# Encoder layer on one core: pool group folded into the output weights, row scales stored in runs of 16 bytes

## What is computed

```
z = rms_norm(x) @ w_in                 # columns: pool group u (512) | q (512) | k | v
# pool group, 4 groups of 128 channels, windows 2/4/8/16
m[g] = centred_mean(u[g]) - u[g]
pool_out[g] = (m[g] @ pool_w[g]) * pool_scale[g]
attn_out = softmax(q k^T / 8) v        # 8 query heads of 64, 2 key heads, q and k normed and rotated
x = x + rms_norm(concat(pool_out, attn_out) @ w_out)
x = x + rms_norm((silu(h @ w_gate) * (h @ w_up)) @ w_down),  h = rms_norm(x)
x = x + (p @ w_ple_proj) * sigmoid(x @ w_ple_gate + b)
```

## Time and profile before

| | us |
|---|---|
| median of 3 runs | 2368.6 |
| lowest, highest | 2368.44, 2368.7 |
| profiled execution, span | 2371.2 |
| attention, first scores to last values | about 395 |

### The profile page before, as it was taken

One profiled execution on the slowest core, in us unless ns is written; L12 is line 12 of the kernel. 1 busy time (PEld: TensorE's weight loads), 2 busy tenths in 40 slices (PEclk: granted clock), 3 DMA queues, 4 the chain that ended last, 5 costly groups with the idle time before them and its releaser, 6 DMA issues.

```text
span 2371.2 us, 29645 instructions
## 1 busy us (share of the span) xinstructions
PE 2305.7 (97%) x10928; PEld 1907.5 (80%) x10928; DVE 1684.8 (71%) x1754; ACT 1038.1 (44%) x1539; POOL 951.7 (40%) x557
## 2 busy tenths in 40 slices
PE   8999999999999989999999999899999999999999
PEld 7888787877778868888887888788788888877877
DVE  5766788888755687676766555888889965575852
ACT  4433788888744453333333222444343333233221
POOL 0000345555423655444443566344456534550210
PEclk9999999999999999999999999999999999999999
DMA  5222233232268884453547867564457587676432
GB/s 198 72 73 97 87 59 74 61 54 59 49 159 246 246 252 161 138 173 122 171 141 262 305 254 263 163 219 163 155 199 260 196 325 265 249 244 236 147 120 75
DMA packets 333550, 402.75 MB, mean 170 GB/s; under 512 B 32736, under 2 KB 236512, under 8 KB 333280
## 3 DMA queue, kind: packets, MB, share of 16 engines
q1 hardware_dynamic: 333408, 400.87, 51.9%
HBM read 259.18 MB, written 137.43 MB: 167 GB/s over the span
## 4 chain that ended last, share of the span: by engine, by line
PE 80%; DVE 8%; DMA 5%; issue 3%; ACT 2%; POOL 1%; SPq 1%; POOLq 0%; DVEq 0%; ACTq 0%
PE ps L1424 46%; PE ps L1213 29%; PE ps L1216 5%; DMA row_scales<-recip 2%; DVE ring L2179 1%; DVE reg L2187 1%; DMA scales<-row_scales 1%; DMA xb<-x_turned 1%; DVE negmax L2083 1%; DMA f_turned<-ev 1%; DVE atb L2097 0%; DVE pt L2125 0%; DVE fhi L2299 0%; DMA ff_forms<-fhi 0%; ACT pt L1529 0%
## 5 line engine op out<-in xcount | busy, mean ns | idle before, releaser
L1424 PE MATMUL ps<-reg,ring 128*128 128x512 f32 x5544 | 1271.0, 391 | 27.0 <-DVE ring L2179 17.7
L1424 PEld LDWEIGHTS ps<-reg,ring 128*128 128x128 f32 x5544 | 1045.5, 189 | 251.2 <-DVE ring L2179 22.0
L1529 ACT ACTIVATE ring<-wraw 128x1024 fp32r<-128x1024 f32 (+2 forms) x152 | 143.7, 946 | 389.5 <-PE ps L1424 389.5
L2179 DVE TENSOR_TENSOR ring<-wraw,ring 128x1024 fp32r<-128x1024 f32 (+2 forms) x152 | 232.2, 1528 | 63.4 <-ACT ring L1529 62.6
L1213 PE MATMUL ps<-win,ht 128*128 128x512 f32 (+1 forms) x1152 | 228.2, 359 | 8.5 <-DVE win L2053 8.3
L1213 PEld LDWEIGHTS ps<-win,ht 128*128 128x128 f32 x1152 | 191.1, 191 | 39.3 <-DVE ht L2010 7.3
L1529 ACT ACTIVATE ring<-ws 128x1024 fp32r<-128x1024 f32 (+2 forms) x114 | 108.0, 947 | 253.3 <-PE ps L1424 236.3
L2179 DVE TENSOR_TENSOR ring<-ws,ring 128x1024 fp32r<-128x1024 f32 (+2 forms) x114 | 175.0, 1535 | 43.2 <-ACT ring L1529 42.6
L2125 DVE TENSOR_TENSOR pt<-ps,pt 128x512 fp32r<-128x512 f32 x256 | 173.6, 685 | 40.5 <-ACT pt L1529 37.6
L1213 PE MATMUL ps<-wout,ct 128*128 128x512 f32 x768 | 180.6, 393 | 2.0 <-DVE wout L2106 1.7
L1529 ACT ACTIVATE pt<-ps 128x512 fp32r<-128x512 f32 x256 | 153.3, 600 | 56.7 <-PE ps L1216 55.9
(11 more groups left out here) (205 smaller groups left out, 2921.4 us busy)
## 6 DMA issues: line engine op xcount, KB each, us to landing
reg<-ff_forms SPq DMA_DIRECT2D x42, 1536.0 KB, 10.0
ff_forms<-fhi SPq DMA_DIRECT2D x88, 512.0 KB, 3.2
wraw<-in_w_gate SPq DMA_DIRECT2D x88, 256.0 KB, 4.2
wraw<-in_w_up SPq DMA_DIRECT2D x88, 256.0 KB, 4.7
ff_forms<-ev SPq DMA_DIRECT2D x44, 512.0 KB, 2.9
wraw<-in_w_down SPq DMA_DIRECT2D x48, 384.0 KB, 5.4
reg<-ff_forms SPq DMA_DIRECT2D x14, 1024.0 KB, 6.8
xt_a<-in_xt SPq DMA_DIRECT2D x16, 512.0 KB, 4.5
```

The lines of the kernel that those rows point to most:

```text
L1424: last = nc.tensor.matmul(ps[:, 2 * chain + m, :], ring[:, st % 3, a, m, k * P:(k + 1) * P], reg[:, k, i, e, :], start=OPENS[i] and k == 0 ...
L1529: copy = lambda out, src, **k: nc.scalar.activation(out, src, ACT.Copy, **k)
L2179: V.tensor_tensor(ring_block(u, st, 1), weight_source(u, i), f(ring_block(u, st, 0)), ALU.subtract).then_inc(S["w_split"], 1)
```

## The change

1. The store of the reciprocals keeps each partition's four values together: `r_d` is (128, 4) in place of (4, 128), so a row is stored in 128 runs of 16 bytes, not 512 of 4 bytes. The order in the row of 512 differs, and `o_scale` reads it with a step of four elements.
2. `pool_w[g]`, times `pool_scale` and turned by the host's layout, is multiplied with rows g of `w_out` once, in the projection (`fold`, g = 0 to 3: two halves of 512 columns, 3 matmuls each, into banks 5 and 6 behind the Q columns of tiles 3 to 6). ACT and DVE split the raw strip (`fold_hi`, `fold_split`), ACT takes the product (`fold_back`), SP loads and stores it in `out_folded`, which the output strips 0 to 3 are then read from.
3. In the attention PE's and ACT's `pooled` and POOL's split are gone; POOL writes the centred mean straight into `plb`.

```diff
@@ misc_schedule
-        order.append(("pool", h))
@@ DRAM
+    wf_d = nc.dram_tensor("out_folded", (NPOOL, P, D), F32, kind="Internal").ap()
-    r_d = nc.dram_tensor("row_scales", (2 * NSEQ * NH, 4, P), F32, kind="Internal").ap()
+    r_d = nc.dram_tensor("row_scales", (2 * NSEQ * NH, P, 4), F32, kind="Internal").ap()
@@ SP
-                sp.dma_start(out_place(k), w_out[k * P:(k + 1) * P, :]).then_inc(S[f"strip_in{k}"], 16)
+                rows = wf_d[k] if k < NPOOL else w_out[k * P:(k + 1) * P, :]
+                sp.dma_start(out_place(k), rows).then_inc(S[f"strip_in{k}"], 16)
+            def fold_in(g):
+                sp.wait_ge(S["strip_split"], KT)
+                sp.wait_ge(S["fold_split"], g)
+                sp.dma_start(fold_raw[:], w_out[g * P:(g + 1) * P, :]).then_inc(S["fold_in"], 16)
                 rows_in(n)
+                if 3 <= n < 3 + NPOOL:
+                    fold_in(n - 3)
+                if 5 <= n < 5 + NPOOL:
+                    sp.wait_ge(S["fold_out"], n - 4)
+                    sp.dma_start(wf_d[n - 5], fold_out[:]).then_inc(S["fold_st"], 16)
-                    sp.dma_start(r_d[hc].rearrange("t p -> p t"), recip[:, hc % 2]).then_inc(on("scales_out"), 16)
+                sp.dma_start(r_d[hc], recip[:, hc % 2]).then_inc(on("scales_out"), 16)
-                sp.dma_start(scales[own_rows(hc)], r_d[hc].rearrange("t p -> (t p)").partition_broadcast(HD))\
+                sp.dma_start(scales[own_rows(hc)], r_d[hc].rearrange("p t -> (p t)").partition_broadcast(HD))\
-                sp.wait_ge(S["misc_free"], MISC[("pool", job)] + 1)
+                sp.wait_ge(S["m_ready"], job + 1)
@@ POOL, windows
-                go(nc.gpsimd.tensor_tensor(m[:, 8:520], s[:, 8:520],
-                                           u[:, PAD + t0:PAD + t0 + 512], ALU.subtract))
-                go(nc.gpsimd.tensor_copy(mt_hl[:, 0, :], m[:, 8:520]))
-                nc.gpsimd.tensor_tensor(mt_hl[:, 1, :], m[:, 8:520], mt_hl[:, 0, :].bitcast(F32),
-                                        ALU.subtract).then_inc(S["m_ready"], 1)
+                pool.wait_ge(*at_least(f"pl_out{hf}", 16 * (job // 2)))
+                nc.gpsimd.tensor_tensor(plb[:, hf], s[:, 8:520],
+                                        u[:, PAD + t0:PAD + t0 + 512], ALU.subtract).then_inc(S["m_ready"], 1)
@@ PE
+            def fold(g):
+                pe.wait_ge(S["fold_split"], g + 1)
+                pe.wait_ge(S["u_stored"], g + 3)
+                pe.wait_ge(S["k_stored"], g + 3)
+                for c in range(2):
+                    for m, (a, b) in enumerate(((0, 0), (0, 1), (1, 0))):
+                        last = mm(ps[:, 5 + c, :], poolw[:, a, g, :], fold_hl[:, b, c * 512:(c + 1) * 512],
+                                  m == 0, m == 2)
+                last.then_inc(S["fold_done"], 1)
                 columns(n, Q)
+                if 3 <= n < 3 + NPOOL:
+                    fold(n - 3)
-                if u == 7:
-                    pooled(h)
@@ ACT
+            def fold_hi(g):
+                act.wait_ge(S["fold_in"], 16 * (g + 1))
+                act.wait_ge(S["fold_done"], g)
+                copy(fold_hl[:, 0], fold_raw[:]).then_inc(S["fold_hi"], 1)
+            def fold_back(g):
+                act.wait_ge(S["fold_done"], g + 1)
+                act.wait_ge(S["fold_st"], 16 * g)
+                copy(fold_out[:], pair(5)).then_inc(S["fold_out"], 1)
                 q_root(n)
+                if 3 <= n < 3 + NPOOL:
+                    fold_back(n - 3)
+                if 2 <= n < 2 + NPOOL:
+                    fold_hi(n - 2)
-                copy(plb[:, half], ps[:, 7, :], scale=pscale[:, k:k + 1]).then_inc(S["misc_free"], 1)
@@ DVE
                 q_rows(n)
+                if 2 <= n < 2 + NPOOL:
+                    dve.wait_ge(S["fold_hi"], n - 1)
+                    V.tensor_tensor(fold_hl[:, 1], fold_raw[:], f(fold_hl[:, 0]), ALU.subtract)\
+                        .then_inc(S["fold_split"], 1)
-                V.tensor_tensor(atb[rows, hc % 2], atb[rows, hc % 2], scales[rows], ALU.mult).then_inc(on("o_scaled"), 1)
+                t = atb[rows, hc % 2].rearrange("p (t n) -> p t n", t=4)
+                V.tensor_tensor(t, t, scales[rows].rearrange("p (n t) -> p t n", t=4), ALU.mult)\
+                    .then_inc(on("o_scaled"), 1)
```

More of the change, by code:

```diff
@@ L564, in scales_through @@
                 sp.wait_ge(*at_least("scales_made", hc + 1))
-                with nc.allow_non_contiguous_dma(reason="512 scales, from columns to a row"):
-                    sp.dma_start(r_d[hc].rearrange("t p -> p t"), recip[:, hc % 2]).then_inc(on("scales_out"), 16)
+                sp.dma_start(r_d[hc], recip[:, hc % 2]).then_inc(on("scales_out"), 16)
             def scales_in(hc):
@@ L1015, in windows @@
                 grp, hf = job % NH // 2, job % 2
+                if job:
+                    pool.wait_ge(S["m_ready"], job)
+                    alone(pool)
                 u = chan[:, grp, :]
@@ L1326, in pv @@
                     last.then_inc(S["pv_done"], 1)
-            def pooled(job):
-                misc(("pool", job))
-                pe.wait_ge(S["m_ready"], job + 1)
-                for m, (a, b) in enumerate(((0, 0), (0, 1), (1, 0))):
-                    last = mm(ps[:, 7, :], poolw[:, a, job % NH // 2, :], mt_hl[:, b, :], m == 0, m == 2)
-                last.then_inc(S["misc_done"], 1)
             turn_q(0, 0)
@@ L1614, in _ @@
                 strip(k)
-            act.wait_ge(S["pw_raw"], 16)
-            copy(poolw[:, 0].rearrange("p g n -> p (g n)"), qtok[:].rearrange("p h d -> p (h d)"))\
-                .then_inc(S["early_hi"], 1)
+            act.wait_ge(S["pw_raw"], 32)
+            raw = qtok[:].rearrange("p h d -> p (h d)")
+            for g in range(NPOOL):
+                last = copy(poolw[:, 0, g], raw[:, g * P:(g + 1) * P], scale=pscale[:, g:g + 1])
+            last.then_inc(S["early_hi"], 1)
             square(0)
@@ L2059, in _ @@
             dve.wait_ge(S["early_hi"], 2)
-            V.tensor_tensor(poolw[:, 1].rearrange("p g n -> p (g n)"),
-                            qtok[:].rearrange("p h d -> p (h d)"),
-                            f(poolw[:, 0]).rearrange("p g n -> p (g n)"), ALU.subtract).then_inc(S["early_lo"], 1)
+            raw = qtok[:].rearrange("p h d -> p (h d)")
+            for g in range(NPOOL):
+                last = V.scalar_tensor_tensor(out=poolw[:, 1, g], in0=raw[:, g * P:(g + 1) * P],
+                                              scalar=pscale[:, g:g + 1], in1=f(poolw[:, 0, g]),
+                                              op0=ALU.mult, op1=ALU.subtract)
+            last.then_inc(S["early_lo"], 1)
             norm(0)
```

92 lines of the change are left out of this document (54 added, 38 removed).

## The result

| | before | after |
|---|---|---|
| median of the runs beside each other | 2368.1 us (7 runs) | 2376.3 us (7 runs) |
| ratio | | 1.0038, 95% interval 1.0028 to 1.0048 |
| profiled execution, span | 2371.2 | 2374.7 |

The change makes the kernel about 9 us slower; 14 us faster had been forecast. On two other chips the ratio came out at 1.0048 and 1.0045, so this is no matter of one chip.

A forecast was written before the change was run, and what follows sets the result against it. PE's own work, and whatever makes DVE late in the attention (`o_scale`), were taken as the bound; 5.5 - 11.2 + 4.2 - 3.7 - 1.7 - 4.0 - 3.2 = -14.1 us, to 2354.5; range 2346 to 2366.

The forecast's parts named there:

- At nothing: List of changes priced at 0, among them small `poolw` passes, loads, semaphores and `o_scale` reading with a step of four.
- The slower rival: `o_scale` on DVE at u = 3 and 7 pays for its step; gain gone from about 0.55 us on; 6%.
- fold, PE's work: Projection: 24 added matmuls of 512 columns at 0.2275 us each on a full PE, +5.5 us.
- fold, waits: Projection: operands and copies have cover and SP's late loads do not reach PE; 0, up to 5 us.
- pooled matmuls: Attention: three matmuls fewer on PE in each of 16 heads, 0.70 us a head, -11.2 us.
- given back at u = 7: Attention: PE, now earlier, waits about 0.28 us for DVE's low part in 15 heads, +4.2 us (0 to 10.5).
- waits behind late DMAs, clock: Attention: two PE waits behind late DMAs go, -3.7 us, and the clock fall near 598 us, -1.7 us.
- collisions with POOL: Attention: POOL's shorter, earlier windows no longer slow `o_scale` at u = 3, -4.0 us (0 to -4.7).
- transition: Into the output projection: waits for the fourth strip and `x1` go, -3.2 us (-1.5 to -3.4).
- the rival that DVE gives back nothing: Attention at u = 7: PE waits the full 0.7 us a head, 6.3 us more, 2360.8 us; 12%.
- The store: Store of the reciprocals in 128 runs of 16 bytes lands in about 5 us in place of 11.15.
- The rival of a store that stays at 11 us: Attention: SP's loop around the long store bounds a half head at 12.0 us; 2364.5 us; 9%.

The follow-up runs named there:

- after_third: The changed kernel, unaltered, timed and profiled on the same chip as the kernel before and a plain-order scales version: ratio to before 1.0045, profiled span 2370.3 us.
- plain_again: Second run, on a third chip, of the changed kernel with `o_scale` reading the scales in plain order (output wrong, same work): ratio to before 1.0000.
- the plain read: The changed kernel with `o_scale` reading the scales in plain order, factors left as stored (output wrong, same work): 2361.3 us, ratio to before 0.9992.
- before_again: The kernel before, unaltered, profiled a second time on another chip: span 2361.8 us, attention 388.5 us in place of 395.5.
- fold_only: The kernel before with the fold and no pooled matmuls in the attention, but the old 4-byte-run store and plain reads: ratio to before 1.0026.
- steps: The changed kernel with eight access patterns of `o_scale` in turn, output wrong, read for lengths alone: 0.68 us with a step of two, 1.10 of four.

## Why the prediction was wrong

The step that failed first is the last clause of "At nothing": **`o_scale` reading with a step of four** was priced at nothing because a step of two is free. It costs 0.40 us each, 11 to 12 us in all (after_third against plain_again: 11.3 at the feed-forward part, 12.2 in the medians). The row said what it said; the step from 8 bytes to 16 was not in it. The slower rival named the right mechanism, place and order of size: its formula with the measured 0.40 gives 16 x 0.2 + 16 x 0.4 = 9.6 us. Its chance, 6%, was low for a cost that no row bounded, and its point of decision, 0.55 us, too late, because the other gains were too large: with 9.6 us it still comes to 2364.1, a gain. And without the step of four the forecast would have been missed too: the plain read is level with before (1.0000), not 14 us under it.

By the pair of traces from one chip (before_again, plain_again, after_third), at the feed-forward part:

| term | forecast | measured |
|---|---|---|
| fold, PE's work | +5.5 | +5.5 |
| fold, waits | 0 (up to 5) | +2.5 to the first scores (2.0 at the first fold); the clock 1.5 more in some executions |
| pooled matmuls | -11.2 | -11.2 (1.40 a pair, where DVE is no bound) |
| given back at u = 7 | +4.2 (0 to 10.5) | +7.9 (0.98 a pair, by a pair of before of 47.35 us, see below) |
| waits behind late DMAs, clock | -3.7, -1.7 | not there in the second trace |
| collisions with POOL | -4.0 | -1.5, what this split leaves of the attention's -4.8 |
| transition | -3.2 | -1.8 |
| step of four | 0 | +11.5 in the attention |
| sum | -14.1 | +12.9 (timed, 0.45%: +10.6) |

*Fold.* The matmuls are right to 0.04 us. The waits were asked for at the wrong place: the text asked when the fold's own operand is ready, and followed SP's queue, and both hold. It never asked what stands behind the wide low part on DVE, which is the next k, its root on ACT, and behind that the copy that empties the fold's bank. What is queued behind a new instruction was followed for the DMAs and not for the compute.

*Pooled matmuls and give-back.* A little disturbed pair of the first trace of before is 47.35 us long, the plain read's 46.94: of 1.40 us off PE 0.41 remains, so 0.49 a head is given back and not 0.28. The bounds (0 to 0.7) held it, and the rival that DVE gives back nothing was as near as the forecast. But before has no steady pair to measure from: those of its first trace run from 47.1 to 53.5 us, most of its second's from 47.4 to 47.9, the latter often with an `o_scale` slowed to between 0.9 and 1.6 us in them. From 47.6 us it would be 0.37 a head and nothing left for the collisions. How the two terms share is therefore not shown; their sum is, +6.4 us (7.9 - 1.5) in place of the forecast +0.2. A slack was read at u = 7 alone. The chain of the plain read (second trace) has `o_scale` on it in both half heads, so at u = 3 there was none left either:

```profile
369.87 0.69 DVE atb L2151
...
381.56 0.69 DVE atb L2151
```

*The store* is right, better than put: 0.6 us of waiting and a median landing of 2.9 us in place of 5. (The 11.15 us taken as its upper bound before was not the longest: the same chain has one of 13.02.) The rival of a store that stays at 11 us is out, and so is its premise: in fold_only the long store stayed, and the pair was 46.96, not the 48 that a loop of 12.0 us would make (4 x 12.0).

*Late DMAs, clock, collisions.* These 9.4 us, two thirds of the forecast, were read off one execution, and in it they were there. In the second they mostly weren't: attention 7.0 us shorter. What the change really removes is smaller: `o_scale` went from a mean of 783 to 682 ns against the plain read, 32 x 0.10 = 3.2 us of DVE, and the pair from about 47.6 (second trace) to 46.94; the attention is 4.8 us shorter (388.5 to 383.7). Of these 4.8 the pooled matmuls account for 3.3 (8 x 0.41) by the split above; the other 1.5 I put down to collisions, without a run that shows it. The short store can have little part in them, since `fold_only`, with the long one, has an attention of 383.8 us.

*Transition.* Last values to feed-forward part: 193.6 us in before's second trace, 191.8, 191.8 and 192.4 in after's three. The wait for `x1` is gone; the one for the fourth strip is 1.25, since DVE's split still waits for its turn there.

*The range.* Its lower end counted on the first trace's waits, its upper end on the rivals up to 9%. A cost for which there is no row should have widened it to the price of its own bound. For an `o_scale` of twice the length 2371 was written and left outside; the forecast's own formula gives 2354.5 + 16 x 0.47 + 16 x 0.67 = 2372.7.

The two traces of before also disprove what the forecast took for granted, that a kernel's one profiled execution is its usual one. Its span of 2371.2 us lay above the highest timed run, 2368.7; that alone was a hint that it held some us which others don't have.

## What to carry to other kernels

- Before a layout change makes an fp32 operand jump, ask whether two consecutive elements still share 16 bytes; with a step of two they did and it was free, with four they didn't and it cost 60%. A DMA saved on one side can be a slower read on the busiest engine on the other; put the strided pass on the engine with slack (here POOL, where it takes 1.55 us: 25 us under the kernel with it on DVE).
- When a loop has a steady pattern, measure the pattern's length, not sums of waits. Equal lengths with and without a piece of work (48.53 us, with or without the pooled matmuls) say which engine sets the pace.
- Waits behind late DMAs and single clock falls belong to an execution; count them as a gain only if a second trace has them.

## What was unexpected in the hardware

- A DVE product of 64 x 512 fp32 takes 0.67 to 0.69 us with steps of one and two elements and 1.04 to 1.14 us with four, eight and sixteen on one operand, or with four on all (run `steps`).
- 128 runs of 16 bytes stored in DRAM land in a median of 2.9 us (1.4 to 7.5, trace of after), with 0.6 us of waiting of SP in all; 512 runs of 4 bytes took 9.2 to 13.4 us where they stood on the chain that ended last in before's two traces, with 34.3 us of waiting in one and 14.4 in the other.
- The same multiplication with the step of four takes 1.55 us on POOL, its plain addition of the same size 1.35.
